# A one-column exponential first, an earlier weight chunk and a new order in the first mixer of a three-layer transformer kernel

## The reference, cut to what matters

```python
h = rms_norm(x, norm_mix_pre[l])
proj = h @ w_in[l]
xr, gr, q, k, v, iq, ik, iw, g_a, g_b = parts          # column ranges of proj
xc = causal_depthwise_conv(xr, conv_w[l], conv_b[l])
y_rnn = rg_lru(xc, ...) * jax.nn.gelu(gr)
y_a = y_rnn @ w_rnn_out[l]
...                                                     # rope on q, k, iq, ik; layer_norm on ik
y_att = dsa_sparse_attention(q, k, v, iq, ik, iw)       # the 64 best keys of each query, then softmax
y_b = y_att @ w_att_out[l]
merged = jax.nn.sigmoid(g_a) * y_a + jax.nn.sigmoid(g_b) * y_b
mix = merged @ w_o[l]
x = x + rms_norm(mix, norm_mix_post[l])
```

## Time and profile before

| | us |
|---|---|
| median of 3 runs | 1411.84 |
| lowest and highest | 1408.5, 1412.55 |
| profiled execution, own time | 1412.74 |
| its span, first to last instruction | 1410.9 |

### The profile page before, as it was taken

The page is one execution under the profiler, slowest core; times in us unless marked ns, Lnnn a source line. Parts: engine busy times, 40 slices in busy tenths (PEclk is TensorE's granted clock), DMA queues, the critical chain, the costliest instruction groups (busy, mean ns, idle before and its releaser), DMA issues.

```text
span 1410.9 us, 18057 instructions
## 1 busy us (share of the span) xinstructions
PE 1388.5 (98%) x6740; PEld 1158.0 (82%) x6740; DVE 885.4 (63%) x1327; ACT 771.7 (55%) x1164; POOL 53.5 (4%) x62
## 2 busy tenths in 40 slices
PE   8999999999999999999999999999999999999999
PEld 7898788788887888888788888888888877888887
DVE  6999856665545655556977555555555594665543
ACT  6679944554545544445866454445444576554441
POOL 2021000000000000000000000000000070000000
PEclk9999999999999999999999999999999999999999
DMA  8544456476665566566346665566655540376651
GB/s 309 176 122 134 152 162 182 133 224 180 192 185 173 176 186 189 182 187 200 111 159 199 190 184 188 185 189 183 189 181 191 158 141 28 120 217 186 190 183 60
DMA packets 127206, 242.55 MB, mean 172 GB/s; under 512 B 7568, under 2 KB 13328, under 8 KB 127120
## 3 DMA queue, kind: packets, MB, share of 16 engines
q1 hardware_dynamic: 126208, 239.15, 55.3%
q0 software_dynamic: 624, 2.10, 0.4%
q10 hardware_dynamic: 288, 0.14, 0.0%
HBM read 240.31 MB, written 1.05 MB: 171 GB/s over the span
## 4 chain that ended last, share of the span: by engine, by line
PE 93%; DVE 4%; ACT 2%; issue 1%; DMA 0%; SPq 0%; ACTq 0%; DVEq 0%
PE PB L347 27%; PE PB L349 27%; PE PB L348 27%; PE PB L393 5%; PE PB L638 2%; PE PB L527 1%; DVE WL L320 1%; PE PB L341 1%; PE PB L343 1%; PE PB L342 1%; ACT WH L314 1%; PE PB L531 0%; DMA X<-in_x_dram 0%; PE PB L1041 0%; PE PB L851 0%
## 5 line engine op out<-in xcount | busy, mean ns | idle before, releaser
L320 DVE TENSOR_TENSOR WL<-RAW,WH 128x1024 fp32r<-128x1024 f32 (+2 forms) x454 | 554.0, 1227 | 438.5 <-ACT WH L314 436.9
L314 ACT ACTIVATE WH<-RAW 128x1024 fp32r<-128x1024 f32 (+2 forms) x454 | 476.2, 1053 | 506.0 <-PE PB L349 494.7
L347 PE MATMUL PB<-WH,AT0h 128*128 128x512 f32 (+3 forms) x1248 | 493.2, 395 | 6.0 <-DVE AT0l L1287 6.0
L349 PE MATMUL PB<-WH,AT0l 128*128 128x512 f32 (+3 forms) x1248 | 482.7, 387 | 0.0
L348 PE MATMUL PB<-WL,AT0h 128*128 128x512 f32 (+3 forms) x1248 | 482.2, 386 | 0.0
L347 PEld LDWEIGHTS PB<-WH,AT0h 128*128 128x128 f32 x1248 | 235.5, 189 | 53.0 <-issue 8.6
L349 PEld LDWEIGHTS PB<-WH,AT0l 128*128 128x128 f32 x1248 | 235.3, 189 | 47.5
L348 PEld LDWEIGHTS PB<-WL,AT0h 128*128 128x128 f32 x1248 | 235.5, 189 | 46.2 <-issue 2.2
L347 PE MATMUL PB<-WH,FTh 128*128 128x512 f32 x440 | 171.9, 391 | 0.0
L349 PE MATMUL PB<-WH,FTl 128*128 128x512 f32 x440 | 171.3, 389 | 0.0
L348 PE MATMUL PB<-WL,FTh 128*128 128x512 f32 x440 | 171.2, 389 | 0.0
(11 more groups left out here) (315 smaller groups left out, 1081.3 us busy)
## 6 DMA issues: line engine op xcount, KB each, us to landing
RAW<-in_ffn_w_gu_dram SPq DMA_DIRECT2D x132, 512.0 KB, 3.7
RAW<-in_ffn_w_gu_2b_dram SPq DMA_DIRECT2D x88, 512.0 KB, 3.7
RAW<-in_w_in_dram SPq DMA_DIRECT2D x44, 512.0 KB, 3.8
RAW<-in_ffn_w_down_dram SPq DMA_DIRECT2D x44, 512.0 KB, 3.3
RAW<-in_ffn_w_down_2b_dram SPq DMA_DIRECT2D x44, 512.0 KB, 3.3
RAW<-in_w_ffn_down_dram SPq DMA_DIRECT2D x22, 512.0 KB, 3.7
RAW<-in_ev_w_in_dram SPq DMA_DIRECT2D x20, 512.0 KB, 3.6
RAW<-in_w_rnn_out_dram SPq DMA_DIRECT2D x8, 512.0 KB, 3.9
```

The lines of the kernel that those rows point to most:

```text
L314: e.activation(WH[i % NHL][:, 0:m], RAW[i % NRAW][:, 0:m], ACT.Copy).then_inc(*up("hi", i))
L320: e.tensor_tensor(WL[i % NHL][:, 0:m], RAW[i % NRAW][:, 0:m], WH[i % NHL][:, 0:m].bitcast(F32), ALU.subtract).then_inc(*up("lo", i))
L347: e.matmul(o, p.src[0][:, kx, t], h[:, j:j + p.n], start=start, stop=False)
L349: ins = e.matmul(o, p.src[1][:, kx, t], h[:, j:j + p.n], start=False, stop=stop)
```

## The change

- ScalarE starts with an exponential of one column of a constant tile of ones (`act_wake`). The memset of ones on POOL becomes a function of its own (`pool_ones`), which still comes first.
- On SP, weight chunk 1 goes ahead of the input's last quarter, chunk 2 stays behind it. PE does the first pass of IQ before it turns that quarter, and ACT and DVE split it after chunks 1 and 2.
- gelu is taken in two visits of four tiles (128 x 1024) each, in place of four of two tiles. `dve_y` waits for the visit that holds its pair.
- The lists of the first mixer on PE, ACT and DVE are in a new order. On POOL two entries change places. Everything after the first mixer is as before.

```diff
+        wake = small(1)
+
+        def act_wake(e):
+
+            e.wait_ge(*on("zero", "ones"))
+            e.activation(wake, ONES[:, 0:1], ACT.Exp).then_inc(*up("warm", "first"))
+
...
-        def act_gelu(e, c, f):
-            t = 4 * c + 2 * f
-            x = GR[:, t:t + 2, :]
-            e.wait_ge(*on("gr_s", t))
-            e.activation(x, x, ACT.Gelu_apprx_tanh).then_inc(*up("evac", ("gr", t)))
+        def act_gelu(e, c):
+
+            x = GR[:, 4 * c:4 * c + 4, :]
+            e.wait_ge(*on("gr_s", 4 * c))
+            e.wait_ge(*on("gr_s", 4 * c + 2))
+            e.activation(x, x, ACT.Gelu_apprx_tanh).then_inc(*up("evac", ("gr", c)))
...
-            e.wait_ge(*on("evac", ("gr", 2 * p)))
+            e.wait_ge(*on("evac", ("gr", p // 2)))
...
             pe_in_turn(e, 2)
+            dense(e, IQ, 0, 1)
             pe_in_turn(e, 3)
-            dense(e, IQ, 0, 6)
-            dense(e, IKW, 0, 5)
+            dense(e, IQ, 1, 6)
+            dense(e, IKW, 0, 4)
             pe_in_spread(e)
-            dense(e, IKW, 5, 6)
+            dense(e, IKW, 4, 6)
             dense(e, KV, 0, 8)
-            dense(e, Q0, 0, 2)
             pe_ik(e)
             pe_iq(e, 0)
-            dense(e, Q0, 2, 4)
+            dense(e, Q0, 0, 2)
...
             sp_x(e, 0)
             load(e, 0)
-            for c in range(1, 4):
-                sp_x(e, c)
-            for i in range(1, 3):
-                load(e, i)
+            sp_x(e, 1)
+            sp_x(e, 2)
+            load(e, 1)
+            sp_x(e, 3)
+            load(e, 2)
...
         def scalar_program(e):
             act_tables(e)
+            act_wake(e)
             act_first_mixer(e)
```

More of the change, by code:

```diff
@@ L658, in build, with pool_ones @@
         iw = small(16)
+        def pool_ones(e):
+            e.memset(ONES, 1.0).then_inc(*up("zero", "ones"))
         def pool_begin(e):
-            e.memset(ONES, 1.0).then_inc(*up("zero", "ones"))
             e.memset(GB[:, :, :], 0.0).then_inc(*up("zero", "bd"))
@@ L2168, in pe_first_mixer @@
             pe_scores(e, AT_A, 5)
-            dense(e, GR0, 9, 12)
+            pe_turn_p(e, AT_A, 3)
+            pe_values(e, AT_A, 2)
+            dense(e, GR0, 8, 9)
             pe_scores(e, AT_A, 6)
[L2171 to L2175, removed]
-            pe_gates(e, 2)
-            pe_turn_p(e, AT_A, 4)
-            pe_values(e, AT_A, 3)
-            dense(e, GR1, 2, 5)
@@ L2180, in pe_first_mixer @@
[L2180 to L2187, removed]
+            pe_scores(e, AT_A, 7)
+            dense(e, GR0, 9, 10)
+            pe_values(e, AT_A, 3)
+            dense(e, GR0, 10, 14)
+            pe_turn_p(e, AT_A, 4)
+            dense(e, GR0, 14, 16)
+            pe_turn_p(e, AT_A, 5)
@@ L2188, in pe_first_mixer @@
+            pe_values(e, AT_A, 4)
+            dense(e, GR1, 0, 1)
+            pe_gates(e, 2)
             pe_turn_q(e, AT_A, 2)
             pe_values(e, AT_A, 5)
-            dense(e, GA0, 5, 7)
+            dense(e, GR1, 1, 4)
+            pe_turn_p(e, AT_A, 6)
             pe_scores(e, AT_A, 8)
+            dense(e, GR1, 4, 5)
+            pe_values(e, AT_A, 6)
+            dense(e, GR1, 5, 16)
+            dense(e, GA0, 0, 1)
+            pe_gates(e, 3)
+            dense(e, GA0, 1, 3)
             pe_scores(e, AT_A, 9)
-            dense(e, GA0, 7, 8)
@@ L2194, in pe_first_mixer @@
             pe_scores(e, AT_A, 10)
-            dense(e, GA1, 0, 2)
-            pe_turn_p(e, AT_A, 6)
-            dense(e, GA1, 2, 4)
+            dense(e, GA0, 3, 4)
             pe_turn_p(e, AT_A, 7)
-            pe_values(e, AT_A, 6)
-            dense(e, GA1, 4, 6)
+            pe_scores(e, AT_A, 11)
+            dense(e, GA0, 4, 5)
             pe_turn_p(e, AT_A, 8)
             pe_values(e, AT_A, 7)
-            pe_scores(e, AT_A, 11)
-            dense(e, GA1, 6, 8)
+            dense(e, GA0, 5, 6)
@@ L2216, in pe_first_mixer @@
             pe_values(e, AT_A, 10)
-            dense(e, GB0, 2, 3)
+            dense(e, GA1, 1, 2)
+            pe_values(e, AT_A, 11)
+            dense(e, GA1, 2, 8)
+            dense(e, GB0, 0, 2)
+            pe_scores(e, AT_A, 14)
+            dense(e, GB0, 2, 4)
             pe_turn_p(e, AT_A, 12)
-            pe_values(e, AT_A, 11)
             pe_scores(e, AT_A, 15)
-            dense(e, GB0, 3, 4)
+            dense(e, GB0, 4, 5)
+            pe_values(e, AT_A, 12)
             pe_turn_p(e, AT_A, 13)
-            pe_values(e, AT_A, 12)
@@ L2530, in act_first_mixer @@
             act_q(e, AT_A, 1)
+            act_exp(e, AT_A, 3)
+            act_p(e, AT_A, 2)
+            act_root(e, 1)
+            act_p(e, AT_A, 3)
             hi(e, 31)
-            act_root(e, 1)
-            act_p(e, AT_A, 2)
+            act_exp(e, AT_A, 4)
+            hi(e, 32)
+            act_exp(e, AT_A, 5)
+            act_p(e, AT_A, 4)
+            act_gr(e, 0, 0)
+            act_gr(e, 0, 1)
+            act_p(e, AT_A, 5)
+            hi(e, 33)
+            act_exp(e, AT_A, 6)
@@ L2552, in act_first_mixer @@
-            act_gelu(e, 0, 1)
-            act_gr(e, 1, 1)
-            hi(e, 37)
-            act_y(e, 1)
-            act_exp(e, AT_A, 5)
-            hi(e, 38)
-            act_gates(e, 3)
-            act_p(e, AT_A, 5)
-            hi(e, 39)
+            act_gates(e, 2)
+            act_q(e, AT_A, 2)
+            act_decay(e, 2)
+            act_p(e, AT_A, 6)
+            hi(e, 34)
+            act_gelu(e, 0)
+            hi(e, 35)
+            hi(e, 36)
+            hi(e, 37)
+            hi(e, 38)
@@ L2561, in act_first_mixer @@
+            act_gr(e, 1, 0)
+            act_y(e, 0)
+            act_gr(e, 1, 1)
+            hi(e, 39)
+            act_gelu(e, 1)
+            act_gates(e, 3)
+            act_exp(e, AT_A, 7)
+            act_exp(e, AT_A, 8)
+            act_exp(e, AT_A, 9)
+            act_p(e, AT_A, 7)
+            act_y(e, 1)
             act_decay(e, 3)
-            act_q(e, AT_A, 2)
+            act_p(e, AT_A, 8)
+            act_exp(e, AT_A, 10)
+            act_exp(e, AT_A, 11)
+            act_p(e, AT_A, 9)
@@ L3339, in pool_program @@
         def pool_program(e):
+            pool_ones(e)
             pool_begin(e)
```

271 lines of the change are left out of this document (122 added, 149 removed).

## The result

The changed kernel takes 1413.18 us in the median (1412.24 to 1415.17, 20 runs) against 1411.86 (1408.5 to 1413.08, 20 runs) of the kernel before. The ratio is 1.0015, interval 1.0008 to 1.0021: about 2 us slower by the ratio, 1.3 by the medians, where 2.1 us less was forecast. It lies at the very edge of the stated range, 1407.0 to 1413.3. Its profiled execution took 1412.32 us, 0.86 under the median.

A forecast was written before the change was run, and what follows sets the result against it. PE, busy 98% of the span, was taken to bound the kernel. Start 0.25 plus old waits 2.18 made 2.4, less a new wait of 0.3 gave 2.1: 1411.84 - 2.1 = 1409.7 us, range 1407.0 to 1413.3.

The forecast's parts named there:

- Start, 0.25 gained: At the wait for the diagonal: one `hi` less ahead gains 0.97, a pass moved ahead costs 0.72, so 0.25 us.
- the upper bound of 0.25 + 0.56: At the start: 0.56 us more than the 0.25 if chunk 6 lands earlier, limited by PE's own arrival at 21.94.
- Old waits, 2.18 gained: PE's waits behind 100 us in the first mixer, 0.81 + 0.55 + 0.82, all go: 2.18 us.
- Against it I keep one new wait of 0.3: First mixer: a reserve of 0.3 us for one new PE wait, because several margins are near 1 us.
- margins of "about 1 us": First mixer: exponentials of units 3, 4 and 5 estimated ready about 1 us before PE asks.
- The slower rival: ACT's queue around `pe_gates(3)`: `act_y(0)`, waiting for DVE, holds the PSUM bank; at worst 1413.3 us; chance 0.13.
- the 1.8 from which that rival decides: Lag of 1.8 us in DVE's `dve_y(0)` beyond which each further us costs PE one us.
- The clock: Stretch at 266.60, where PE ran 3.80 us at granted clock 0.55, keeps full speed: 1.7 us; its rival's chance 0.1.

The follow-up runs named there:

- the start alone: Kernel before with only the change of the start, up to the first ten weight casts, mixer as before; 1410.69 us, ratio 0.9997.
- after: The changed kernel itself, as seen in its profiled execution of 1412.32 us; median 1413.18 us, ratio 1.0015 to the kernel before.
- the small product: Changed kernel with POOL's two products of GR1 cut from 256 to 8 columns of each tile; 1411.97 us, ratio 1.0001.
- gelu(1) late: Changed kernel with gelu(1) moved on ACT from ahead of gates(3) to ahead of the first tanh of GA; 1409.73 us, ratio 0.9986.
- max(7) early: Changed kernel with DVE's max(7) and max(8) moved from behind y(1) to behind y(0) and ylo(0); 1410.37 us, ratio 0.9985.
- two-operand instruction added: Changed kernel with a one-column DVE TENSOR_TENSOR of two SBUF operands added behind y(0) and behind ylo(0); 1411.87 us, ratio 1.0005.
- one-operand twin: Changed kernel with a one-column DVE TENSOR_SCALAR of one SBUF operand added behind y(0) and behind ylo(0); 1411.96 us, ratio 1.0006.
- three casts as STT: Changed kernel with DVE's subtractions of weight chunks 37 to 39 written as SCALAR_TENSOR_TENSOR, same operands and order; 1412.94 us, ratio 1.0012.
- after's second execution: The changed kernel profiled once more with no edit; 1412.62 us, ratio 1.0012.
- the mixer's order alone: Changed kernel with the old start and the rest of the mixer as changed; 1413.31 us, ratio 1.0017.

## Why the prediction was wrong

Forecast 1409.7, measured 1413.18.

- **Start, 0.25 gained.** Right in kind, and in size as far as shown: 0.21 in the kernel with the start alone, 0.99 in after, over the upper bound of 0.25 + 0.56. What came on top is the scatter of chunk 6's landing, which the old start has as well. PE's first product came at 8.39, not 9.2, since x had landed 1.4 us earlier; none of that is seen in the chain at the diagonal, which waits for chunk 6. ACT's first split was held for the constants (2.17 us), not seen coming, and cost nothing.
- **Old waits, 2.18 gained.** Right. None is left, the first reciprocal of `dve_out` runs at 108.25 instead of 115.88, and there are 9 table loads.
- **"Against it I keep one new wait of 0.3".** This step failed. There are two new ones, 1.02 and 2.94. The margins of "about 1 us" were laid for units 3, 4 and 5 alone; neither the scores of unit 3, whose bank max(1) frees behind gx(0), nor unit 7 was laid. gx(0) took 1.54 us there instead of the 0.68 that the same instruction takes at 100.08 us, again beside a product of POOL.
- **The slower rival** named the right queue: act_y(0), the copy, hi(39), gelu(1), gates(3) and unit 7's exponential, and that gelu(1) "also waits for POOL". It named the wrong holder. DVE was on time: act_y(0) waited 0.72 us and held the copy up by 0.4, under the 1.8 from which that rival decides. What failed is that POOL's product was priced at its 1.35 us of the earlier trace rows, and the blocking only in one direction, DVE standing still for POOL. That POOL could be kept out for 5 us was not thought of; both its products took 7.61 us. The time, 1413.3, was met for another reason.
- **The clock** was asked about at 266.60 only. There it stayed as it was (0.60 from 268 to 272 us of after); it fell behind the new wait as well, in two of the four executions that have it.

A rule that points at the failed step was at hand. The section of the Trainium skill that the prediction named (Advanced Engine Details and Errata, "Mode Summary") says of VectorE's two-port modes alone that they and GpSimd block each other. The Trainium skill (SBUF — State Buffer, "SBUF: two separate sides") says that a VectorE instruction with two SBUF inputs contends with a GpSimd one that reads SBUF, that the one that starts first has the port for its whole length, and that the other blocks fully. That the wait goes both ways agrees with the trace of the small product, 5.29 us for 16 columns. But by this rule POOL waits for the rest of one DVE instruction, here at most 1.2 us; that the wait can go on over several it doesn't say, and in before it didn't (below). So the rule alone would not have given the 5 us.

The cause is shown by gelu(1) late (the queue) and by max(7) early (POOL's opening), each removing the wait alone. That the two new waits and the slow clock make up the whole loss is shown to about 1 us, the scatter of the medians.

## What to carry to other kernels

When an order is laid anew, lay out each engine that someone waits for, the idle one too: a product on POOL that takes 1.3 us can stand for 5 more beside a DVE that goes from product to product. Don't put an instruction that waits for a third engine in front of what the bounding engine needs next; moved behind it, the same late product cost nothing. A list's shorter work (5 us of table loads here) is worth nothing where its queue stands still.

## What the runs showed of the hardware

- POOL's wait here was not for one DVE instruction but for a run of them. Between 126.22 and 131.4 us there are five seams of DVE products of 512 to 1024 columns, and POOL, ready since 126.3, got into none, whether they were TENSOR_TENSOR or SCALAR_TENSOR_TENSOR. It got in ahead of an instruction that reads PSUM, in a stop of 0.17 us, and ahead of a one-column instruction with one or with two SBUF operands. The seam between the cast of chunk 37 and ylo(0), which stayed shut in after, let the second product in with max(7) early: it was ready at 128.92, ended at 131.06, and ylo(0) took 1.75 us beside it. With the two-operand instruction added the same seam stayed shut for it, ready at 127.90. What decides stays open, for in the kernel before POOL got in at the very next seam between two such DVE instructions, of 512 and 1024 columns (POOL, then DVE; the cast takes 1.22 us alone):

```profile
125.35 1.56 POOL L732 TENSOR_TENSOR GR<-GR,JK 128x512 f32<-128x512 f32 x1 [11.85 <-ACT GR L725]
```
```profile
125.07 0.69 DVE L901 SCALAR_TENSOR_TENSOR T<-T 128x512 f32<-128x512 f32 x1
125.68 2.31 DVE L320 TENSOR_TENSOR WL<-RAW,WH 128x1024 fp32r<-128x1024 f32 x1
```

- Once in, POOL cost DVE mostly about a us at a meeting, in before too (2.31 for 1.22 above): ylo(0) 1.75 for 0.69, a cast 2.26 for 1.22, one column 1.28 where its one-operand twin took 0.15. It cost 0.3 where a mask addition and a maximum ran beside most of it (1.53 for 1.22, with max(7) early).
- The same wait of 2.8 us without a matmul was followed by a granted clock of 0.55 over the next 3 us (after), of 0.60 (three casts as STT) and twice of 1.00 (after's second execution, the mixer's order alone).
